# Seven weight slots laid out with high and low part side by side, each starting 64 bytes further modulo 512

## The chip, the cores and the metric

The kernel runs on one core of a Trainium2 chip. The metric is the device time of one execution in microseconds (us). Three runs of the kernel before gave 1726.82, 1725.1 and 1726.75 us, median 1726.75 us.

## The reference, cut to what matters

Two model blocks of two layers each work on one sequence of 256 tokens with 1024 channels in float32. Almost all the work is the product of activations with weight matrices that are used once each:

```python
for l in range(DEPTH):                       # first block
    proj = x @ w_in[l]
    ...                                      # recurrent mixer and sparse attention
    mix = jnp.concatenate([o_a, o_b], axis=-1) @ w_out[l]
    x = layer_norm(ALPHA * x + mix, ln1_g[l], ln1_b[l])
    ffn = (jax.nn.silu(x @ w_ffn_gate[l]) * (x @ w_ffn_up[l])) @ w_ffn_down[l]
    x = layer_norm(ALPHA * x + ffn, ln2_g[l], ln2_b[l])
```

The second block has the same outline, with three kinds of attention, gated branches (`gates[:, :, 0] * (o_mla @ w_branch[0]) + ...`), a feed-forward part with a short convolution, and a last gate.

## The kernel before, in words

**Weights as a stream.** All weights are cut into units of 128 partitions x 1024 float32 values, in the order in which they are used. A ring of seven slots (`RING`, L37) holds them. SyncE loads unit u into slot u mod 7 of `raw` (L625). ScalarE writes its high part, rounded to fp32r, to `w_hi` (L682). VectorE, for five slots of seven, and GpSimd, for two, write the low part `raw - w_hi` to `w_lo` (L686). A slot is 4096 bytes of a partition in each of the three tensors.

**Each product three times.** Activations are kept in a high and a low part too (`x_t_hi` and `x_t_lo`, and likewise `o_t`, `hs`, `n_t`, `c_t`, `pe`). TensorE adds high x high, high x low and low x high in PSUM. Every matmul of this kernel is a weight load (LDWEIGHTS, the stationary operand, 128 columns) and a matmul that streams the moving operand past it. There are two forms:

- `feature_major` (matmul on L720): the weights are stationary, 128 columns of a slot; the moving operand is a 256-column slice of `x_t` or `o_t`. 24 matmuls for a unit.
- `token_major` (matmul on L737): the activations are stationary; the moving operand is the weight slot, mostly 512 columns at a time. 12 matmuls for a unit.

```python
for k, (a, b) in enumerate(((w_hi, hi), (w_lo, hi), (w_hi, lo))):
    ...
    for kt in range(n, n + 4):
        mm = pe.matmul(target, a[:, i, w0 + kt * P:w0 + (kt + 1) * P], b[:, k0 + kt, :],
```

A feed-forward part runs gate and up units feature-major with `x_t` and down units token-major with `hs` as the stationary operand. The first matmul of a unit releases an older slot to ScalarE (`unit_begun`), and a finished low part releases the slot of `raw` to the next load. This order of work is written out by hand, and the change leaves it alone.

**Where things lie.** `sb` (L312) gives each tensor the next address of the partition, rounded up to 64 bytes. `raw`, `w_hi`, `w_lo`, `x`, 32 bytes of padding (L331), `x_t_hi`, `x_t_lo`, 32 bytes of padding (L334), then the constants and all others follow each other. A slot is 4096 bytes, so all seven slots, high and low, begin at one and the same address modulo 512. Every slice that the two forms of matmul read inside a slot (but for those of the 416- and 280-column units) and inside an activation tensor also begins a whole multiple of 512 bytes further. Counted from the weight slots and modulo 512, `x_t` lies at 32, `o_t` at 128, and `hs`, `n_t`, `c_t` and `pe` at 256.

In each form the address of the moving operand less that of the stationary one, modulo 512, is called the distance here. Before the change it is one number for a pair of tensors:

| matmul | moving less stationary |
|---|---|
| L720, `x_t` over weights | 32 |
| L720, `o_t` over weights | 128 |
| L737, weights over `x_t` | 480 |
| L737, weights over `o_t` | 384 |
| L737, weights over `hs`, `n_t`, `c_t`, `pe` | 256 |

Of the kernel before, what the change touches and what calls it, by code (L numbers as in the profile page):

```python
# [19 lines left out]
F32R = mybir.dt.float32r  # L20
# [4 lines left out]
P = 128  # L25
# [11 lines left out]
RING = 7  # L37
UNIT = 1024
# [264 lines left out]
def program(nc, stream, x_in, consts_in, onehot_in, rb_in, flip_in, param1_in, rows1_in,  # L303
# [5 lines left out]
    with ctx:  # L309
        top = [nc.sbuf_base + (-nc.sbuf_base) % 64]  # L310

        def sb(name, shape, dtype=F32, at=None):  # L312

            size = 4 * int(np.prod(shape[1:]))
            if at is None:
                at = top[0]
                top[0] += size + (-size) % 64
            assert at + size <= nc.sbuf_usable_end, (name, at + size)
            return nc.alloc_sbuf_tensor_at(name, shape, dtype, offset=at)
# [5 lines left out]


        raw = sb("raw", [P, RING, UNIT])
        w_hi = sb("w_hi", [P, RING, UNIT], F32R)
        w_lo = sb("w_lo", [P, RING, UNIT], F32R)
        x = sb("x", [P, T, D])  # L330
        top[0] += 32  # L331
        x_t_hi = sb("x_t_hi", [P, KT, S], F32R)
        x_t_lo = sb("x_t_lo", [P, KT, S], F32R)
        top[0] += 32  # L334
        consts = sb("consts", [P, N_CONST])
        ones = sb("ones", [P, P])
        mean_ones = sb("mean_ones", [P, P])
# [2630 lines left out]
```

## Time and profile before

| | us |
|---|---|
| median of 3 runs | 1726.75 |
| the profiled execution, its own time | 1727.11 |
| span of that execution | 1725.3 |
| TensorE matmul busy | 1653.6 (96%) |
| TensorE weight load busy | 1504.2 (87%) |
| VectorE busy | 1170.4 (68%) |
| ScalarE busy | 921.4 (53%) |
| GpSimd busy | 441.4 (26%) |

The profile's page gives busy time, shares of the chain that ended last, and groups of equal instructions. TensorE's matmuls overlap in the records: a matmul's own duration includes the time that its results take to drain, so durations add up to more than the span. The pace of a stream of matmuls is read from the timeline, as the difference of two start times divided by the number of matmuls that start in between.

### The profile page before, as it was taken

What the parts mean: (1) busy time and instruction counts of PE and PEld (TensorE: products, weight loads), DVE (VectorE), ACT (ScalarE), POOL (GpSimd) and SP (SyncE); (2) the same over time, 40 slices, a digit from 0 to 9 for tenths busy, and PEclk for the clock granted to TensorE, in tenths of its full rate; (3) what the DMA queues carried; (4) which work ended last, traced back from release to release, by engine and by line L of the source; (5) the groups of instructions that cost most, each with busy time, mean ns of one, the idle gap of its engine ahead of it and who ended that gap; (6) DMA issues with size and microseconds to landing.
All of it is one profiled execution on the core that took longest, in us unless ns stands there. A gap on an engine that the chain in (4) does not pass through costs nothing.

```text
span 1725.3 us, 30143 instructions
## 1 busy us (share of the span) xinstructions
PE 1653.6 (96%) x11354; PEld 1504.2 (87%) x11354; DVE 1170.4 (68%) x1601; ACT 921.4 (53%) x1576; POOL 441.4 (26%) x184
## 2 busy tenths in 40 slices
PE   8989999999988999999999999999999999999997
PEld 6878799989887899978899989999788999899996
DVE  5687754467786545476884877666767856777677
ACT  5664554446645544465655564545755555554445
POOL 2212122212121322224511132222235211222222
PEclk9999999999999999999999999999999999999999
DMA  9432455646523665546333455655554333466653
GB/s 332 157 119 96 161 199 185 201 147 210 162 78 122 220 193 188 191 153 213 113 110 100 140 199 184 215 185 182 180 194 146 110 100 116 161 218 199 207 183 127
DMA packets 82563, 288.74 MB, mean 167 GB/s; under 512 B 9051, under 2 KB 11908, under 8 KB 81924
## 3 DMA queue, kind: packets, MB, share of 16 engines
q1 hardware_dynamic: 77352, 272.58, 48.1%
q10 hardware_dynamic: 5084, 14.37, 2.5%
q8 instruction: 91, 1.49, 0.4%
q14 instruction: 36, 0.29, 0.1%
HBM read 284.81 MB, written 2.11 MB: 166 GB/s over the span
## 4 chain that ended last, share of the span: by engine, by line
PE 62%; DVE 7%; ACT 3%; issue 2%; DVEq 0%; ACTq 0%
PE bank L720 30%; PE bank L737 25%; PE bank L1294 2%; DVE w_lo L686 2%; PE bank L1275 1%; PE bank L1266 1%; ACT w_hi L682 1%; PE bank L765 1%; PE bank L1254 1%; PE bank L1307 0%; DVE qk L2528 0%; PE bank L1186 0%; PE bank L774 0%; PE bank L910 0%; DVE z L2502 0%
## 5 line engine op out<-in xcount | busy, mean ns | idle before, releaser
L686 POOL TENSOR_TENSOR w_lo<-raw,w_hi 128x1024 fp32r<-128x1024 f32 x146 | 375.3, 2570 | 1175.7 <-ACT w_hi L682 1175.7
L686 DVE TENSOR_TENSOR w_lo<-raw,w_hi 128x1024 fp32r<-128x1024 f32 x364 | 558.2, 1558 | 153.9 <-ACT w_hi L682 151.5
L682 ACT ACTIVATE w_hi<-raw 128x1024 fp32r<-128x1024 f32 x510 | 520.0, 1052 | 101.6 <-PE bank L737 46.3
L720 PE MATMUL bank<-x_t_hi,w_hi 128*128 128x256 f32 x1984 | 321.4, 284 | 5.3 <-ACT gl L1430 2.9
L720 PE MATMUL bank<-x_t_hi,w_lo 128*128 128x256 f32 x1984 | 313.9, 280 | 0.0
L720 PE MATMUL bank<-x_t_lo,w_hi 128*128 128x256 f32 x1984 | 313.5, 280 | 0.0
L720 PEld LDWEIGHTS bank<-x_t_hi,w_hi 128*128 128x128 f32 x1984 | 273.9, 190 | 16.8 <-issue 5.1
L720 PEld LDWEIGHTS bank<-x_t_hi,w_lo 128*128 128x128 f32 x1984 | 268.7, 189 | 0.0
L720 PEld LDWEIGHTS bank<-x_t_lo,w_hi 128*128 128x128 f32 x1984 | 268.2, 189 | 0.0
L737 PE MATMUL bank<-w_hi,x_t_hi 128*128 128x512 f32 (+3 forms) x448 | 136.1, 387 | 9.4 <-issue 5.8
L737 PE MATMUL bank<-w_hi,x_t_lo 128*128 128x512 f32 (+3 forms) x448 | 133.5, 381 | 1.5 <-DVE x_t_lo L1962 1.5
L737 PE MATMUL bank<-w_lo,x_t_hi 128*128 128x512 f32 (+3 forms) x448 | 133.2, 380 | 0.0
L737 PE MATMUL bank<-w_hi,hs_hi 128*128 128x512 f32 x352 | 109.4, 392 | 4.0 <-ACT hs_hi L1875 4.0
L737 PE MATMUL bank<-w_lo,hs_hi 128*128 128x512 f32 x352 | 108.9, 390 | 0.0
L737 PE MATMUL bank<-w_hi,hs_lo 128*128 128x512 f32 x352 | 108.7, 390 | 0.0
L737 PEld LDWEIGHTS bank<-w_hi,x_t_hi 128*128 128x128 f32 x448 | 81.2, 191 | 31.0 <-issue 14.0
L737 PEld LDWEIGHTS bank<-w_hi,x_t_lo 128*128 128x128 f32 x448 | 82.4, 190 | 19.3 <-DVE x_t_lo L1962 3.4
L737 PEld LDWEIGHTS bank<-w_lo,x_t_hi 128*128 128x128 f32 x448 | 83.1, 191 | 16.3
L1871 ACT ACTIVATE gs<-cv 128x256 f32<-128x256 f32 x44 | 18.4, 419 | 145.9 <-DVE cv L2676 145.9
L737 PEld LDWEIGHTS bank<-w_lo,hs_hi 128*128 128x128 f32 x352 | 66.1, 188 | 14.6
L737 PEld LDWEIGHTS bank<-w_hi,hs_lo 128*128 128x128 f32 x352 | 66.1, 188 | 14.3
L2363 DVE TENSOR_TENSOR hs_lo<-hs,hs_hi 128x256 fp32r<-128x256 f32 x36 | 15.3, 425 | 86.6 <-ACT hs_hi L1654 86.6
(390 smaller groups left out, 2128.0 us busy)
## 6 DMA issues: line engine op xcount, KB each, us to landing
raw<-stream SPq DMA_DIRECT2D x511, 512.0 KB, 4.3
rows<-rows ACTq DMA_DIRECT2D x4, 1024.0 KB, 4.6
gain<-rows ACTq DMA_DIRECT2D x8, 512.0 KB, 4.6
hv_p<-hv_dram ACTq DMA_DIRECT2D x14, 256.0 KB
x<-x_in SPq DMA_DIRECT2D x2, 512.0 KB, 5.0
bias_r<-rev_dram SPq DMA_DIRECT2D x1, 1024.0 KB, 7.3
hv_dram<-hv ACTq DMA_DIRECT2D x2, 512.0 KB, 7.4
y_out<-x SPq DMA_DIRECT2D x2, 512.0 KB, 2.7
```

Of the source, the lines that this page charges most:

```text
L682: self.eng.activation(w_hi[:, i, :], raw[:, i, :], ACT.Copy).then_inc(hi_done.sem, 1)
L686: self.eng.tensor_tensor(w_lo[:, i, :], raw[:, i, :], w_hi[:, i, :].bitcast(F32), ALU.subtract).then_inc((lo_pool if self.part == "pool" e ...
L720: mm = pe.matmul(target, a[:, i, w0 + kt * P:w0 + (kt + 1) * P], b[:, k0 + kt, :], start=kt + k == 0, stop=k == 2 and kt == kts - 1)
L737: mm = pe.matmul(target, a[:, kt0 + j, t * P:(t + 1) * P], b[:, i, j * width + c0:j * width + c0 + cn], start=first and j + k == 0, stop=l ...
L765: mm = pe.transpose(b[:, k * P:(k + 1) * P], source[:, t, (4 * h + k) * P:(4 * h + k + 1) * P], ident)
L1254: mm = pe.matmul(bank[banks.bank(at, f"s{i + half}")][:, t * S:(t + 1) * S], q[:, t * P:(t + 1) * P], k, start=True, stop=True)
L1266: mm = pe.matmul(b[:, t * S:(t + 1) * S], mq_t[:, h, t * P:(t + 1) * P], mk_t[:, h, :], start=True, stop=True)
L1275: mm = pe.transpose(b[:, m * P:(m + 1) * P], z2[:, i % 4, m * P:(m + 1) * P], ident)
L1294: mm = pe.matmul(bank[b0 + t][:, o], p_t2[:, i % 2, m * P:(m + 1) * P], v, start=kk == 0, stop=kk == 1)
L1871: act.activation(gs2[:, i % 2, :], cv[:, i % 2, :], ACT.Gelu_apprx_tanh).then_inc(c["gate_silu"].sem, 1)
L2363: dve.tensor_tensor(hs_lo[:, i % TAIL, :], hs[:, i % 2, :], hs_hi[:, i % TAIL, :].bitcast(F32), ALU.subtract).then_inc(c["h_lo"].sem, 1)
```

## The change

```diff
         raw = sb("raw", [P, RING, UNIT])
-        w_hi = sb("w_hi", [P, RING, UNIT], F32R)
-        w_lo = sb("w_lo", [P, RING, UNIT], F32R)
+        w = sb("w", [P, RING, 2 * UNIT + 16], F32R)
+        w_hi, w_lo = w[:, :, 0:UNIT], w[:, :, UNIT:2 * UNIT]
         x = sb("x", [P, T, D])
-        top[0] += 32
         x_t_hi = sb("x_t_hi", [P, KT, S], F32R)
         x_t_lo = sb("x_t_lo", [P, KT, S], F32R)
-        top[0] += 32
         consts = sb("consts", [P, N_CONST])
```

A slot now holds 4096 bytes of high part, 4096 bytes of low part and 64 bytes of nothing, so that slot i begins 64 x i bytes further modulo 512. `x` moves up by 448 bytes, `x_t` by 416, all that follows by 384. `raw` stays. No instruction is added, removed or moved; only addresses differ. The distances become:

| matmul | moving less stationary, slots 0 to 6 |
|---|---|
| L720, `x_t` over weights | 448, 384, 320, 256, 192, 128, 64 |
| L720, `o_t` over weights | 0, 448, 384, 320, 256, 192, 128 |
| L737, weights over `x_t` | 64, 128, 192, 256, 320, 384, 448 |
| L737, weights over `o_t` | 0, 64, 128, 192, 256, 320, 384 |
| L737, weights over `hs`, `n_t`, `c_t`, `pe` | 384, 448, 0, 64, 128, 192, 256 |

## Rows read from the trace of the kernel before

**Rows 1.** The page: busy time, and the granted clock in 40 slices.
```profile
PE 1653.6 (96%) x11354; PEld 1504.2 (87%) x11354; DVE 1170.4 (68%) x1601; ACT 921.4 (53%) x1576; POOL 441.4 (26%) x184
...
PEclk9999999999999999999999999999999999999999
```

**Rows 2.** The page: shares of the chain that ended last, by engine.
```profile
PE 62%; DVE 7%; ACT 3%; issue 2%; DVEq 0%; ACTq 0%
```

**Rows 3.** Groups by line, TensorE: xcount | busy us, mean ns | idle before.
```profile
L720 PE MATMUL bank<-x_t_hi,w_hi 128*128 128x256 f32 x1984 | 321.4, 284 | 5.3 <-ACT gl L1430 2.9 <-ACT p_t L549 1.6 <-ACT x_t_hi L1419 0.7
L720 PE MATMUL bank<-x_t_hi,w_lo 128*128 128x256 f32 x1984 | 313.9, 280 | 0.0
L720 PE MATMUL bank<-x_t_lo,w_hi 128*128 128x256 f32 x1984 | 313.5, 280 | 0.0
L737 PE MATMUL bank<-w_hi,x_t_hi 128*128 128x512 f32 (+3 forms) x448 | 136.1, 387 | 9.4 <-issue 5.8 <-DVE w_lo L686 2.4 <-ACT x_t_hi L1419 0.8
...
L737 PE MATMUL bank<-w_hi,hs_hi 128*128 128x512 f32 x352 | 109.4, 392 | 4.0 <-ACT hs_hi L1875 4.0
...
L720 PE MATMUL bank<-o_t_hi,w_hi 128*128 128x256 f32 x192 | 30.9, 283 | 0.4 <-DVE o_t_lo L2394 0.3
```

**Rows 4.** Timeline at 600 us, TensorE: start us, us, what; L720 with x_t.
```profile
600.06 0.63 PE L720 MATMUL bank<-x_t_hi,w_lo 128*128 128x256 f32 x4
...
602.40 0.28 PE L720 MATMUL bank<-x_t_hi,w_hi 128*128 128x256 f32 x1
```

**Rows 5.** Timeline at 960 us, TensorE: L720 with o_t.
```profile
960.11 0.64 PE L720 MATMUL bank<-o_t_lo,w_hi 128*128 128x256 f32 x4
...
962.49 0.28 PE L720 MATMUL bank<-o_t_hi,w_lo 128*128 128x256 f32 x1
```

**Rows 6.** The chain that ended last in order of time: start us, us, what.
```profile
953.37 34.47 PE bank L720 x288
...
1176.09 16.80 PE bank L720 x144
```

**Rows 7.** Timeline at 1000 us, TensorE: L737 with x_t stationary.
```profile
999.80 0.63 PE L737 MATMUL bank<-w_hi,x_t_lo 128*128 128x512 f32 x2
...
1002.60 0.63 PE L737 MATMUL bank<-w_hi,x_t_lo 128*128 128x512 f32 x2
```

**Rows 8.** Timeline at 186 us, TensorE: L737 with o_t stationary.
```profile
186.16 0.62 PE L737 MATMUL bank<-w_hi,o_t_hi 128*128 128x512 f32 x2
...
188.96 0.39 PE L737 MATMUL bank<-w_hi,o_t_hi 128*128 128x512 f32 x1
```

**Rows 9.** Timelines at 1519 and 1012 us, TensorE: L737 with hs and pe stationary.
```profile
1519.55 0.62 PE L737 MATMUL bank<-w_lo,hs_hi 128*128 128x512 f32 x2
...
1521.83 0.63 PE L720 MATMUL bank<-x_t_hi,w_hi 128*128 128x256 f32 x4
...
1011.86 0.62 PE L737 MATMUL bank<-w_hi,pe_lo 128*128 128x512 f32 x2
...
1014.58 0.62 PE L737 MATMUL bank<-w_hi,pe_lo 128*128 128x512 f32 x2
```

**Rows 10.** Timeline at 836 us, TensorE: short matmuls, dv over p_t.
```profile
836.73 1.06 PE L1294 MATMUL bank<-dv,p_t 128*128 128x128 f32 x8
837.63 0.60 PE L1186 MATMUL bank<-consts,sqn 128*128 128x128 f32 x4
```

**Rows 11.** Instructions of tile w_hi: xcount: duration ns min/median/max, first and last start.
```profile
L682 ACT ACTIVATE w_hi<-raw x510: 1037/1047/1109, 6.6 to 1719.8; 128x1024 fp32r<-128x1024 f32 x170
...
L686 DVE TENSOR_TENSOR w_lo<-raw,w_hi x364: 1209/1225/3456, 7.7 to 1721.6; 128x1024 fp32r<-128x1024 f32 x182
...
L686 POOL TENSOR_TENSOR w_lo<-raw,w_hi x146: 2352/2454/3417, 11.8 to 1721.0; 128x1024 fp32r<-128x1024 f32 x146
```

## The prediction, written before the changed kernel had run

> **What bounds the kernel now.** The page first. TensorE's matmuls are busy for 1653.6 us of 1725.3 us, at a granted clock whose 40 slices all read 9, so nearly always the 2.4 GHz level [rows 1]. The chain that ended last is mostly TensorE, 62% of the span, with 12% on other engines and on issue [rows 2]. So what each of TensorE's streaming matmuls takes more or less reaches the end nearly whole, while time won on VectorE, ScalarE or GpSimd reaches it only through the few waits. Next the groups by line. L720 with `x_t` runs 3 x 1984 = 5952 matmuls of 256 columns; L737 runs 3 x 448 = 1344 with `x_t` stationary (1056 of them 512 columns wide, the rest narrower) and 3 x 352 = 1056 with `hs` stationary; L720 with `o_t` runs 3 x 192 = 576 [rows 3]. The reader should see how many there are: 1 ns on each of the 5952 is 6.0 us, 0.35% of the time.
>
> The change moves addresses and nothing else, so it can act only if the pace of an instruction depends on where its operands lie. The trace of before shows five distances between moving and stationary operand, and paces for them (start to start, over a run of matmuls that wait for nothing else):
>
> - L720, `x_t`, distance 32: 20 matmuls in 602.40 - 600.06 = 2.34 us, 117.0 ns [rows 4]; 144 in 16.80 us, 116.7 ns [rows 6].
> - L720, `o_t`, distance 128: 20 in 2.38 us, 119.0 ns [rows 5]; 288 in 34.47 us, 119.7 ns, which holds the changes of bank too [rows 6].
> - L737, distance 480: 12 in 2.80 us, 233.3 ns [rows 7].
> - L737, distance 384: 12 in 2.80 us, 233.3 ns [rows 8].
> - L737, distance 256: 10 in 2.28 us, 228.0 ns with `hs`, and 12 in 2.72 us, 226.7 ns with `pe` [rows 9].
>
> The same shape on the same engine takes 2 ns more or 6 ns more between these rows. Address is one thing in which they differ, the producer of the stationary tensor and the stage another. I take the address to be the likelier reason, since the shapes are equal and the streams wait for nothing.
>
> **The change part by part.**
>
> *L720 with `x_t`, 5952 matmuls.* The distance goes from 32 to 64, 128, 192, 256, 320, 384 and 448, a seventh of the units each. Only 128 has a row: 2.0 ns above distance 32 (119.0 less 117.0) [rows 4, 5]. The bounds are both ends of what rows show: all seven stay at 117.0, nothing; all seven come to 119.0, 5952 x 2.0 = +11.9 us. Below that, a distance could be better than 32: the floor is then the pace of a matmul that is short enough to leave only the weight load, 8 in 837.63 - 836.73 = 0.90 us, 112.5 ns [rows 10], and all seven there would be 5952 x 4.5 = -26.8 us. I take the middle between the two rows for this same form, +1.0 ns: 5952 x 1.0 = +6.0 us.
>
> *L737 with `x_t` stationary, 1056 wide matmuls.* From 480 to 64, 128, ... 448. Of the seven, 256 has 227 ns and 384 has 233 ns; 448 lies between two distances that both have 233 ns (384 and 480), so 233; the four others have no row and get the middle, 230. Mean (227 + 2 x 233 + 4 x 230) / 7 = 230.4 ns, 2.9 ns below now: 1056 x 2.9 = -3.1 us. Bounds: nothing, and -6.6 x 1056 = -7.0 us if all reach 226.7.
>
> *L737 with `hs` stationary, 1056 matmuls.* These lie at 256 now, the best distance that a row shows, and go to 384, 448, 0, 64, 128, 192 and 256. By the same figures (0 counted as unknown) the mean is (2 x 233 + 227 + 4 x 230) / 7 = 230.4 ns, against 228.0: 1056 x 2.4 = +2.5 us. Bounds: nothing, and +5.3 x 1056 = +5.6 us.
>
> *Distance 0.* Slot 2 over `hs`, and slot 0 with `o_t`, now begin together modulo 512. The short matmuls of `dv` over `p_t` have both operands at 384 modulo 512, distance 0, and run at 112.5 ns [rows 10]. So I price no special penalty for it.
>
> *The remaining matmuls on weights* (`o_t`, `n_t`, `c_t`, `pe` and the narrow ones, some 1300) start from 128, 256, 384 and 480 and land on the same mixture: zero, with 2 ns x 1300 = 2.6 us to either side.
>
> *ScalarE, VectorE and GpSimd on the slots.* They read `raw`, which stays, and write `w_hi` and `w_lo` at new addresses. ScalarE's 510 take 1037 to 1109 ns, VectorE's have minimum 1209 and median 1225 ns for the same 1024 elements [rows 11]; the long ones are GpSimd and VectorE in each other's way, which does not hang on addresses. Cost zero. TensorE is the cover: GpSimd and VectorE are idle for 74% and 32% of the span [rows 1]. If VectorE's 364 each took 50 ns more, 18 us of its time, nearly all would lie under TensorE.
>
> *Loads.* `raw` and the source stay where they are, so the 511 stream loads are unchanged. The transposes of `x` over the identity matrix come to distance 0; there are 64 and the row above speaks for no change.
>
> **Sum.** +6.0 - 3.1 + 2.5 = +5.4 us, of which some 90% lie on the path (where TensorE waits for another engine anyway, its pace is free): +4.9 us. The profiled execution took 1727.11 us, 0.36 us above the median of the three runs, so I forecast 1726.75 + 4.9, about 1731.5 us, 0.3% slower. The measurement can tell about 0.2%, 3.5 us, from no change, so this is a small effect close to that border.
>
> **The rivals.**
>
> *Rival A, faster: spreading gets most slots out of each other's way.* Weight load and moving stream of TensorE disturb each other only near certain distances, and 32 is one of them; 117.0 against the 112.5 ns of the short ones would be the price paid now. With the slots spread over seven distances, five in seven run at 112.5 ns: 5952 x 4.5 x 5/7 = -19.1 us, and the wide matmuls over `x_t` gain 3 us, `hs` loses 2.5: about 1707 us. For it: 112.5 ns is what the weight load alone needs, so 4.5 ns are there to be explained. Against it: distance 128 is a row of before and is slower, not faster, than 32 [rows 4, 5], and 226.7 against 233.3 ns shows that wide streams differ by distances which are all multiples of 64 or near one. Milder forms (two slots in seven gain) give 1718 us. Chance 0.3.
>
> *Rival B, no change: pace does not depend on the distance.* Then the differences between rows come from stage and form. For it: ScalarE and VectorE show flat durations whatever TensorE reads [rows 11], and distance 0 costs nothing at 112.5 ns [rows 10]. The time stays within 3 us of 1726.75. Chance 0.32. The Trainium skill speaks for this rival and so against any effect of the change: in "TensorE: Matmul & The Clock Gate", section "What happens when you issue a matmul", the weight load and the moving operand have SBUF read ports of their own, and loading the next weights takes nothing from the running matmul; "SBUF — State Buffer", section "Who interferes with whom", adds that TensorE waits on nobody. By that rule the sum would be 0. The rows do not settle it: equal shapes at 226.7 and 233.3 ns ask for some cause that the rule leaves no room for.
>
> *Rival C, clearly slower: what matters is the remainder modulo 64.* `x_t` lies 32 bytes off a multiple of 64 now and would come to rest on one, like `o_t`. All 5952 would take 119.0 ns: +11.9 us, and the wide ones over `x_t` would stay at 233, with `hs` unchanged at 228: 1739 us. It decides as soon as the offset of 32 is what makes `x_t` quicker than `o_t`. For it: `x_t` is the only moving operand off a multiple of 64, and it has the quickest 256-column row. Chance 0.15, part of the slower cases.
>
> **How the numbers follow.** Forecast with its neighbourhood (slower by over 3.5 us, up to 8 us) 0.23, Rival A 0.3, Rival B 0.32, Rival C 0.15. The forecast is the sum's own value; since cases of both signs hold most of the chance and the effect is small, the likeliest one's own range is 1729 to 1736 us. The range reaches from Rival A in its strong form, a little below 1707, to the bounds of the slower terms added, 11.9 + 5.6 = 17.5 us above now: 1704 to 1744 us. Outside stays a gain on all slots (1700 or less) or a penalty at a distance that no row shows. Faster by over 0.2%: 0.30. Within 0.2%: 0.32. Slower by over 0.2%: 0.38.
>
> **What the profile of the changed kernel would show.** The timeline of L720 with `x_t` should run at different paces in units of different slots, 117 to 119 ns, mean 118; equal paces of 117 in all units mean Rival B, 112 to 114 in most mean Rival A, 119 in all mean Rival C. L737 over `x_t` should come from 233 to about 230 ns, L737 over `hs` go from 228 to about 230 ns. Durations of L682 and L686, counts of instructions and the granted clock should not move. The prediction is wrong if the time moves without the pace of L720, for instance through waits of TensorE on L686, or if one slot alone (slot 2 over `hs`) carries the loss.

## The result, and the profile after

| | before | after |
|---|---|---|
| median of 10 runs, us | 1726.78 | 1733.25 |
| span of the profiled execution, us | 1725.3 | 1731.2 |
| TensorE matmul busy, us | 1653.6 | 1659.2 |

The ratio is 1.0038, with a 95% interval of 1.0028 to 1.0047: the changed kernel is 6.5 us slower by the medians. The forecast was 1731.5 us.

The page of the changed kernel, busy time, granted clock and the chain, against [rows 1, 2]:

```profile
PE 1659.2 (96%) x11354; PEld 1507.2 (87%) x11354; DVE 1168.7 (68%) x1601; ACT 921.0 (53%) x1576; POOL 440.9 (25%) x184
...
PEclk9999999999999999999999999999999999999999
...
PE 63%; DVE 7%; ACT 2%; issue 2%; DVEq 0%; ACTq 0%
```

Counts of instructions and the clock's digits are as they were; the mean granted clock was 0.986 before and 0.988 after. VectorE, ScalarE and GpSimd are busy for 0.4 to 1.7 us less; TensorE alone is busy for longer, by 5.6 us, and the span is longer by 5.9 us. Names are shorter now (`w` for both parts) and lines two lower: L718 is the old L720, L735 the old L737.

Six feed-forward units in a row, L718 with `x_t`, in the changed kernel's timeline of TensorE (start us, us, what). The units begin at 1181.36, 1184.22, 1187.05, 1189.90, 1192.72 and 1195.45 us and use slots 3, 4, 5, 6, 0 and 1:

```profile
1181.36 1.11 PE L718 MATMUL bank<-x_t_hi,w 128*128 128x256 f32 x8
...
1184.22 1.11 PE L718 MATMUL bank<-x_t_hi,w 128*128 128x256 f32 x8
...
1187.05 1.11 PE L718 MATMUL bank<-x_t_hi,w 128*128 128x256 f32 x8
...
1189.90 1.10 PE L718 MATMUL bank<-x_t_hi,w 128*128 128x256 f32 x8
...
1192.72 1.07 PE L718 MATMUL bank<-x_t_hi,w 128*128 128x256 f32 x8
...
1195.45 1.10 PE L718 MATMUL bank<-x_t_hi,w 128*128 128x256 f32 x8
...
1198.29 0.63 PE L735 MATMUL bank<-w,hs_hi 128*128 128x512 f32 x2
```

A unit is 24 matmuls, so each difference divided by 24 is a pace: 119.2 ns at distance 256, 117.9 at 192, 118.8 at 128, 117.5 at 64, 113.8 at 448, 118.3 at 384. Same instructions, same engine, no wait between them, and paces from 113.8 to 119.2 ns in units of different slots. In [rows 4] 20 matmuls ran at 117.0. The down units follow suit. One over `hs` at distance 384 and one at 64:

```profile
591.07 1.09 PE L735 MATMUL bank<-w,hs_hi 128*128 128x512 f32 x4
...
593.86 1.11 PE L718 MATMUL bank<-x_t_hi,w 128*128 128x256 f32 x8
...
599.54 1.09 PE L735 MATMUL bank<-w,hs_hi 128*128 128x512 f32 x4
...
602.30 1.07 PE L718 MATMUL bank<-x_t_hi,w 128*128 128x256 f32 x8
```

2.79 us and 2.76 us for 12 matmuls, 232.5 and 230.0 ns, against 228.0 in [rows 9].

Below, "mean pace" is the mean difference between the starts of two successive matmuls of a form on the same pair of tensors in the whole trace, where gaps more than 60 ns above the streaming time (over 167 ns for 256 columns, over 273 ns for 512) are left out: waits, and the stretches at the 1.2 GHz level, where a matmul of 256 columns starts every 213 to 214 ns. By it, the change did this:

| form | matmuls | before, ns | after, ns | us |
|---|---|---|---|---|
| L720, `x_t` | 5952 | 116.8 | 117.7 | +5.4 |
| L737, `x_t`, 512 wide | 1056 | 233.3 | 231.6 | -1.9 |
| L737, `hs` | 1056 | 228.5 | 231.7 | +3.4 |
| sum | | | | +6.9 |

The last column is matmuls times difference, from paces before rounding. The changes of all other matmuls on weights cancel to less than 0.1 us. The pace of TensorE's matmuls accounts for the whole 6.5 us.

Runs of one kernel scatter by several us, and the granted clock goes with it: of the ten runs of the changed kernel the two with a mean clock of 0.990 took 1731.3 and 1731.4 us, and the one with 0.983 took 1736.7 us. Over 93 runs that list a clock (the changed kernel, the experiments with several runs, and the kernel before beside them), a clock lower by 0.001 goes with 0.6 us more inside one kernel (an estimate, by a straight line through them).

### The profile page after: what moved, and what is told of

It is laid out like the page before. It is cut to its first block, busy times and chain, and to the rows that moved or that the text cites. A ratio compares the mean times of both kernels' runs of the same rounds, so it can differ in the third digit from the quotient of the medians.

```text
span 1731.2 us, 30143 instructions
## 1 busy us (share of the span) xinstructions
PE 1659.2 (96%) x11354; PEld 1507.2 (87%) x11354; DVE 1168.7 (68%) x1601; ACT 921.0 (53%) x1576; POOL 440.9 (25%) x184
## 4 chain that ended last, share of the span: by engine, by line
PE 63%; DVE 7%; ACT 2%; issue 2%; DVEq 0%; ACTq 0%
PE bank L718 30%; PE bank L735 25%; DVE w L684 2%; PE bank L1292 2%; PE bank L1273 1%; PE bank L1264 1%; ACT w L680 1%; PE bank L763 1%; PE bank L1252 1%; PE bank L1305 0%; DVE qk L2526 0%; PE bank L908 0%; PE bank L916 0%; PE bank L1184 0%; PE bank L772 0%
## 5 line engine op out<-in xcount | busy, mean ns | idle before, releaser
L684 POOL TENSOR_TENSOR w<-raw,w 128x1024 fp32r<-128x1024 f32 x146 | 374.9, 2568 | 1184.6 <-ACT w L680 1184.6
L684 DVE TENSOR_TENSOR w<-raw,w 128x1024 fp32r<-128x1024 f32 x364 | 556.9, 1554 | 154.7 <-ACT w L680 152.8
L680 ACT ACTIVATE w<-raw 128x1024 fp32r<-128x1024 f32 x510 | 520.1, 1052 | 105.7 <-PE bank L735 45.3
L718 PE MATMUL bank<-x_t_hi,w 128*128 128x256 f32 x3968 | 556.7, 283 | 5.3 <-ACT gl L1428 3.0
L718 PEld LDWEIGHTS bank<-x_t_hi,w 128*128 128x128 f32 x3968 | 509.1, 189 | 17.7 <-issue 5.4
L718 PE MATMUL bank<-x_t_lo,w 128*128 128x256 f32 x1984 | 314.7, 281 | 0.0
L718 PEld LDWEIGHTS bank<-x_t_lo,w 128*128 128x128 f32 x1984 | 269.0, 189 | 0.0
L735 PE MATMUL bank<-w,x_t_hi 128*128 128x512 f32 (+3 forms) x896 | 232.6, 382 | 9.6 <-issue 5.8
L735 PEld LDWEIGHTS bank<-w,x_t_hi 128*128 128x128 f32 x896 | 162.7, 191 | 46.2 <-issue 14.2
L735 PE MATMUL bank<-w,hs_hi 128*128 128x512 f32 x704 | 192.1, 394 | 3.7 <-ACT hs_hi L1873 3.7
L735 PEld LDWEIGHTS bank<-w,hs_hi 128*128 128x128 f32 x704 | 127.2, 188 | 28.2 <-issue 4.0
L735 PE MATMUL bank<-w,x_t_lo 128*128 128x512 f32 (+3 forms) x448 | 132.7, 379 | 1.7 <-DVE x_t_lo L1960 1.7
L735 PE MATMUL bank<-w,hs_lo 128*128 128x512 f32 x352 | 109.7, 393 | 0.0
L735 PEld LDWEIGHTS bank<-w,x_t_lo 128*128 128x128 f32 x448 | 82.3, 190 | 19.5 <-DVE x_t_lo L1960 4.0
L735 PEld LDWEIGHTS bank<-w,hs_lo 128*128 128x128 f32 x352 | 66.1, 188 | 15.5
L718 PE MATMUL bank<-o_t_hi,w 128*128 128x256 f32 x384 | 53.6, 282 | 0.7 <-DVE o_t_lo L2392 0.7
L718 PEld LDWEIGHTS bank<-o_t_hi,w 128*128 128x128 f32 x384 | 48.8, 189 | 1.1 <-DVE o_t_lo L2392 1.1
```

Of the source, the lines that this page charges most:

```text
L680: self.eng.activation(w_hi[:, i, :], raw[:, i, :], ACT.Copy).then_inc(hi_done.sem, 1)
L684: self.eng.tensor_tensor(w_lo[:, i, :], raw[:, i, :], w_hi[:, i, :].bitcast(F32), ALU.subtract).then_inc((lo_pool if self.part == "pool" e ...
L735: mm = pe.matmul(target, a[:, kt0 + j, t * P:(t + 1) * P], b[:, i, j * width + c0:j * width + c0 + cn], start=first and j + k == 0, stop=l ...
```

## The experiments

The theory: the pace depends on the distance between the operands' addresses, and on little else that the change touches. Every run changes addresses alone, by padding. `rest` stands for all tensors behind `x_t`.

**High and low part side by side, without the stagger.**

```diff
-        w_hi = sb("w_hi", [P, RING, UNIT], F32R)
-        w_lo = sb("w_lo", [P, RING, UNIT], F32R)
+        w = sb("w", [P, RING, 2 * UNIT], F32R)
+        w_hi, w_lo = w[:, :, 0:UNIT], w[:, :, UNIT:2 * UNIT]
```

> High and low part side by side, but without the 64 bytes of stagger and with both paddings of 32 bytes kept, so that every distance (moving less stationary operand, modulo 512) is that of the kernel before. Theory of distances: the pace of L720 with x_t stays at 116.8 ns and the time at 1726.8 us, within 2 us. Rival (the slot's layout itself costs the time, by the 28672 bytes from high to low part that become 4096, or by what ScalarE and VectorE write): the whole loss of the change, 1733 us, shows here.

Measured: 1727.6 us against 1727.35 us for the kernel before on the same chip, ratio 1.0001 (0.9992 to 1.0010). Mean paces 116.8, 233.4 and 228.5 ns, those of before. The new layout of a slot costs nothing that these runs can tell (the interval stays within 1.7 us); the stagger and the paddings taken out, that is the distances, carry the loss.

**One other distance for all slots.** In the next three runs only the two paddings around `x_t` change, so that `x_t` moves and the rest stays at its place modulo 512.

```diff
         x = sb("x", [P, T, D])
-        top[0] += 32
+        top[0] += 192
         x_t_hi = sb("x_t_hi", [P, KT, S], F32R)
         x_t_lo = sb("x_t_lo", [P, KT, S], F32R)
-        top[0] += 32
+        top[0] += 384
```

> The kernel before with x_t put 192 bytes behind the weight slots modulo 512 instead of 32, all else at its old place modulo 512. In the changed kernel the units at distance 192 had the quickest pace of L720 with x_t, 115.4 ns, and those of L737 over x_t at 320 had 230.5 ns. Theory of distances: 5952 x (115.4 - 116.8) = -8.3 us and 1056 x (230.5 - 233.3) = -3.0 us, so 1715.5 us, faster than both kernels. Rival (unequal slots disturb each other through their sequence, not through the distance of each): the pace does not follow, and the time stays within 3 us of 1726.8.

Measured: 1723.84 us against 1727.35, ratio 0.9984 (0.9974 to 0.9993). It is faster than both kernels, but by a third of what was expected. L737 over `x_t` came to 229.2 ns, better than expected; over `hs`, whose distance had not changed, to 226.8 from 228.5; L720 over `x_t` stayed at 116.8 ns, where 115.4 had been expected. The unit means show why: of the 248 units with this distance some run at 114 ns a matmul and more at 118, and few between (single matmuls: 23% at 113 or 114 ns, 67% at 117 or 118). The changed kernel's 115.4 ns had been such a mixture too, with more of the quick ones.

> The same with x_t 256 bytes behind the slots. In the changed kernel the units at distance 256 had the slowest pace of L720 with x_t, 119.7 ns, and 229.8 ns in L737 over x_t. Theory of distances: 5952 x (119.7 - 116.8) = +17.3 us, 1056 x (229.8 - 233.3) = -3.7 us, so 1740.4 us. Rival as for the run before: 1726.8 us, within 3.

(paddings 256 and 320.) Measured: 1736.93 us, ratio 1.0056 (1.0042 to 1.0070), slower by 9.6 us. L720 over `x_t` 119.8 ns as expected, in 9 of 10 matmuls exactly 120; L737 over `x_t` 227.5 ns, better than the 229.8 expected.

> The same with x_t 160 bytes behind the slots, like the 32 of the kernel before no multiple of 64. Theory that the pace is a smooth function of the distance modulo 512: L720 with x_t lies between the 118.5 ns of distance 128 and the 115.4 ns of 192, at about 117 ns, and the time at 1726 us, within 4. Rival C of the prediction (what matters is being 32 bytes off a multiple of 64): 116.8 ns exactly as at distance 32, and all multiples of 64 alike, which the changed kernel's paces from 115.4 to 119.7 ns already speak against.

(paddings 160 and 416.) Measured: 1736.12 us, ratio 1.0050 (1.0036 to 1.0064). L720 over `x_t` 118.6 ns, L737 233.5 ns. Both readings fail. 160 is 32 off a multiple of 64 and yet slow, which rules Rival C out. And the pace is not about 117 ns, between its neighbours 128 (118.5 ns) and 192 (115.4 ns) in the changed kernel, but as slow as the slower of them.

The chain in order of time shows these paces in one row each, because it holds the same stretch in every kernel: 144 matmuls of L720 with `x_t`, and 96 of L737 over `x_t`. The kernel at distance 192, then the one at 256 and the one at 160 (start us, us, what):

```profile
986.49 21.99 PE bank L737 x96
...
1176.23 16.96 PE bank L720 x144
```

```profile
996.62 21.80 PE bank L737 x96
...
1186.92 17.27 PE bank L720 x144
```

```profile
995.70 22.41 PE bank L737 x96
...
1185.58 17.09 PE bank L720 x144
```

144 matmuls take 16.96 us (117.8 ns; this stretch ran at the slower of the two paces of distance 192), 17.27 us (119.9) and 17.09 us (118.7), against 16.80 us in [rows 6].

**Does the place itself count, or other engines' addresses?**

```diff
         raw = sb("raw", [P, RING, UNIT])
+        top[0] += 192
         w_hi = sb("w_hi", [P, RING, UNIT], F32R)
```

> 192 bytes of padding ahead of w_hi in the kernel before, so that every tensor but raw lies 192 bytes further and no distance on TensorE changes. Theory of distances: pace of L720 with x_t 116.8 ns, of L737 over x_t 233.3 ns, time 1727 us. Rival (what counts is where an operand itself begins modulo 512, or where ScalarE and VectorE write against what they read from raw): other paces, at the least 1 ns off on L720, and L682 or L686 of other durations.

One run took 1729.68 us, where the kernel before took 1730.38 us beside it. Mean paces 116.9, 233.3 and 228.5 ns. ScalarE's and VectorE's durations on the slots, in the view of tile `w_hi`, are those of [rows 11] within 2 ns but for VectorE's longest; GpSimd's median is 27 ns longer:

```profile
L683 ACT ACTIVATE w_hi<-raw x510: 1037/1047/1111, 6.5 to 1722.5; 128x1024 fp32r<-128x1024 f32 x170
...
L687 DVE TENSOR_TENSOR w_lo<-raw,w_hi x364: 1207/1225/3467, 7.6 to 1724.3; 128x1024 fp32r<-128x1024 f32 x182
L687 POOL TENSOR_TENSOR w_lo<-raw,w_hi x146: 2378/2481/5143, 12.4 to 1723.6; 128x1024 fp32r<-128x1024 f32 x146
```

A common shift of both operands by 192 bytes changes no pace, while 64 bytes between them do: of the two, it is the difference between TensorE's operands that counts. Other common shifts were not tried by themselves.

**The period.**

> x_t 288 bytes behind the slots, 256 more than before. If the pattern repeats every 512 bytes (what the stagger supposes), the pace of L720 with x_t is free to be any; if it repeats every 256 bytes, as the changed kernel's paces at 64 and 320 (117.5 and 117.7 ns) and at 128 and 384 (118.5 and 118.7 ns) suggest, it is 116.8 ns as at 32, L737 over x_t 233.3 ns, and the time 1727 us.

(paddings 288 and 288.) 1727.83 us in one run, against 1730.38 us beside it. Mean paces 116.8, 233.3 and 228.5 ns: those of distance 32 to the last digit. For this distance 256 bytes more change nothing, so the pattern seems to repeat every 256 bytes, not only every 512. The slots of the changed kernel mostly agree: over `x_t` 117.5 and 117.7 ns at 64 and 320, 118.5 and 118.6 ns at 128 and 384. At 192 and 448 they had 115.4 and 117.2 ns, mixtures of two paces in which 192 had more quick units (23 of 38 against 6 of 36). The chain's rows of this kernel are those of before, 16.80 and 22.39 us:

```profile
988.62 22.39 PE bank L737 x96
...
1176.90 16.80 PE bank L720 x144
```

Seven slots staggered by 64 bytes thus use only four distances: in L720 over `x_t`, two slots each at 64, 128 and 192, and one at 0.

> x_t 96 bytes behind the slots. Smooth theory: between 117.5 ns (64) and 118.5 ns (128) on L720, 118 ns, about 1732 us. Rival C (32 bytes off a multiple of 64 is what helps): 116.8 ns. Distance 160 had 118.6 ns, so Rival C is expected to fail here too.

(paddings 96 and 480.) 1746.63 us in one run, against 1730.38 us for the kernel before beside it; span 1744.8 us, 19.5 us longer than that of the profile before. It is the slowest distance found. L720 120.1 ns, in single matmuls anything from 116 to 125; L737 over `x_t` 234.3 ns, over `hs` 229.9 ns. Both expectations miss: it is worse than either neighbour.

```profile
1190.50 17.28 PE bank L720 x144
```

> x_t 224 bytes behind the slots, between the 116.8 ns that distance 192 had in a kernel with one distance for all and the 119.8 ns of 256. Smooth theory: 118.3 ns on L720 and 228 to 229 ns on L737 over x_t, about 1731 us. If distances of the form 32 below a multiple of 256 behave as 32 above one does (two streams that pass each other at the same lag), 116.8 ns and about 1722 us.

(paddings 224 and 352.) 1736.84 us in one run, against 1730.38 us beside it. L720 118.3 ns as the smooth theory had it; L737 over `x_t` 233.3 ns instead of 228 to 229.

**Half steps.** All paddings so far are multiples of 32 bytes. For steps of 16 the slots themselves were put 16 bytes into a larger tensor, with paddings 128 and 384 for the first of the two runs and 160 and 352 for the second.

```diff
-        w_hi = sb("w_hi", [P, RING, UNIT], F32R)
-        w_lo = sb("w_lo", [P, RING, UNIT], F32R)
+        w = sb("w", [P, 2 * RING * UNIT + 16], F32R)
+        w_hi, w_lo = (w[:, a:a + RING * UNIT].rearrange("p (i n) -> p i n", i=RING) for a in (4, 4 + RING * UNIT))
```

> Weight slots begin 16 bytes later, x_t 176 bytes behind them, 16 below the 192 at which the units of L720 turned out to run in one of two states, 113 to 114 or 118 ns a matmul, apparently set when a unit begins. hs comes to distance 272, o_t to 112. If the lag between weight load and stream decides which state holds, a distance beside 192 may hold the quick one: 114 ns, 5952 x (114 - 116.8) = -16.7 us on L720, about 1708 us. Smooth theory: between 118.6 ns (160) and 116.8 ns (192), 117.7 ns, and about 1730 us.

1739.3 us in one run, against 1730.45 us for the kernel before beside it; L720 over `x_t` 118.7 ns, over `hs` (distance 272) 231.7 ns.

> The same with x_t 208 bytes behind the slots, 16 above 192. Quick state held: 114 ns on L720, about 1708 us. Smooth theory: between 116.8 ns (192) and 118.3 ns (224), 117.5 ns, and about 1729 us.

1742.76 us in one run, against the same 1730.45 us; L720 over `x_t` 119.0 ns, L737 over `x_t` 233.3 ns, over `hs` 231.8 ns. Neither holds the quick state, and both are slower than the smooth theory said. The idea that a distance beside 192 fixes the quick state is wrong for these two. (Both move the slots by 16 bytes and `hs` to distance 272 as well, so their times are not those of `x_t` alone.)

**Only `hs` and `o_t` moved.**

```diff
         x_t_lo = sb("x_t_lo", [P, KT, S], F32R)
-        top[0] += 32
+        top[0] += 96
```

> The kernel before with the second padding 96 instead of 32 bytes, so that everything behind x_t moves by 64 and x_t stays: L737 over hs comes from distance 256 to 192, L720 with o_t from 128 to 192. The changed kernel's units over hs at 192 had 233.5 ns, those of o_t at 192 had 116.8 ns. Theory of distances, with additive terms: 1056 x (233.5 - 228.5) = +5.3 us and 576 x (116.8 - 118.8) = -1.2 us, L720 with x_t at 116.8 ns as before, time 1731 us, slower by 0.24%. Rival (the loss of the changed kernel came from x_t alone, the paces over hs were an echo of it): 1727 us, over hs 228.5 ns.

Measured: 1734.14 us against 1726.16 us, ratio 1.0038 (1.0025 to 1.0052). Over `hs` 232.7 ns (+4.3 ns, +4.5 us), L720 with `o_t` 115.5 ns from 118.8 (-1.9 us), L720 over `x_t` 116.8 as before. A down unit of this kernel:

```profile
1104.86 0.62 PE L737 MATMUL bank<-w_hi,hs_hi 128*128 128x512 f32 x2
...
1107.64 0.63 PE L720 MATMUL bank<-x_t_hi,w_hi 128*128 128x256 f32 x4
```

12 in 2.78 us, 231.7 ns, against 228.0 in [rows 9]. So the term over `hs` is real without any move of `x_t`. The time lost, 6.6 us by the ratio, is more than the 2.3 us of these paces (4.5 less 1.9, less 0.3 for L737 over `o_t`); `n_t`, `c_t` and `pe`, which moved too, add 0.9 us. Part of the rest goes with the clock: the five runs had a mean granted clock of 0.9854, the 14 of before that count 0.9881, worth 1.6 us by the estimate above. In the profiled execution some single waits of TensorE differ by about 1 us from those of before, both ways: longer at 103 (`hid`), 174 (`am`), 490 (`q_e`) and 1474 us (`o_t`), shorter at 753 (`x_t`) and 951 us (transposes of `o`). What decides these isn't settled; several of them appear in the kernel below too, which is faster. In sum TensorE was not busy for 75.5 us of the span here, and for 71.7 us before.

**The version that the paces point to.** `x_t` at 192, `o_t` at 192 (448), `hs` at 256.

```diff
         x = sb("x", [P, T, D])
-        top[0] += 32
+        top[0] += 192
...
-        top[0] += 32
+        top[0] += 128
         consts = sb("consts", [P, N_CONST])
...
+        top[0] += 64
         o_base = top[0]
         o_t_hi = sb("o_t_hi", [P, 12, S], F32R)
         o_t_lo = sb("o_t_lo", [P, 12, S], F32R)
+        top[0] += 192
         dist = sb("dist", [P, T, S])
```

> The best version that the paces point to: x_t 192 bytes behind the slots as in the run of 1723.8 us, o_t at 448, which by the period of 256 is 192 again, hs at 256. Theory of distances: L720 with x_t 116.8 ns, L737 over x_t 229.2 ns, over hs 226.8 ns, L720 with o_t from 118.8 to 116.8 ns (-1.2 us), so 1722.7 us, 0.2% below the kernel before. If o_t adds nothing: 1723.8 us. If units with x_t stay in their quick state of 113 to 114 ns, more, down to 1705 us, but nothing here is made to hold it.

Measured: 1724.96 us against 1726.16, ratio 0.9984 (0.9973 to 0.9995), the same as with `x_t` alone. L720 over `o_t` ran at 113.4 ns, the quick state in nearly all units, 5.4 ns below before where 2 were expected; its timeline:

```profile
955.15 0.62 PE L722 MATMUL bank<-o_t_hi,w_lo 128*128 128x256 f32 x4
...
957.42 0.62 PE L722 MATMUL bank<-o_t_hi,w_hi 128*128 128x256 f32 x4
```

20 matmuls in 2.27 us, 113.5 ns. Over 576 matmuls that is 3.1 us, and little of it arrives. The chain in order of time says where it goes. Before, this stretch was one piece, 288 matmuls in 34.47 us from 953.37 to 987.84 us [rows 6]. Now:

```profile
954.57 16.62 PE bank L722 x144
971.20 0.02 issue
971.22 0.43 DVE merged_b L2627
971.64 1.69 DVE merged L2632
...
981.51 2.35 DVE w_lo L688 x2
983.86 0.33 DVE merged L2627
984.20 2.30 DVE x_t_lo L2614
...
986.89 1.65 PE bank L722 x12
988.54 11.67 PE bank L739 x51
```

In the middle of the stretch the chain leaves TensorE for VectorE, which merges the branches and splits weights and is now the later of the two. The stretch takes 988.54 - 954.57 = 33.97 us, 0.50 us less than before, for 288 x 5.4 ns = 1.56 us of quicker matmuls.

Over the whole kernel two more things eat into the gain. In this profiled execution TensorE was not busy for 77.1 us of the span (76.1 us in that with `x_t` alone at 192), against 71.7 us before. And the granted clock was lower: 0.9847 on the average of the 11 runs against 0.9881 for the kernel before, worth 2.0 us by the estimate above. One of its drops in the timeline:

```profile
1031.50 0.79 PE L739 MATMUL bank<-w_hi,hs_hi 128*128 128x512 f32 x2 [2.29 <-ACT hs_hi L1877]
1032.09 1.05 PE L739 MATMUL bank<-w_lo,hs_hi 128*128 128x512 f32 x2
1032.95 1.05 PE L739 MATMUL bank<-w_hi,hs_lo 128*128 128x512 f32 x2
1033.80 1.05 PE L739 MATMUL bank<-w_hi,hs_hi 128*128 128x512 f32 x2
```

TensorE has waited 2.29 us, the granted clock from 1032.0 to 1035.4 us is 0.50, the level of 1.2 GHz, and a matmul starts every 425 ns. In the kernel before the same unit follows a wait of 2.00 us, the clock stays at 1.00, and the pace is 225 ns. In all, the matmuls on weights in such stretches took 12.8 us more here than they would have at the upper level, against 10.3 us before (an estimate, with 117, 173, 190 and 230 ns for the widths 256, 384, 416 and 512). Whether the change of addresses brings these drops about, by moving the waits, was not tested.

**All distances, in one table** (modulo 256, mean pace in kernels with one distance for all slots; `x_t` is the activation unless another is named):

| distance | L720, 256 columns, ns | L737, 512 columns, ns |
|---|---|---|
| 0 | 119.8 | 226.8 to 230.1 (`hs`), 227.5 (`x_t`) |
| 16 | | 231.7 and 231.8 (`hs`) |
| 32 | 116.8 | 233.3 |
| 48 | | 233.3 |
| 64 | | 229.2 |
| 80 | | 231.1 |
| 96 | 120.1 | 233.5 |
| 112 | 120.0 and 118.4 (`o_t`) | |
| 128 | 118.8 (`o_t`) | 232.4 (`o_t`) |
| 160 | 118.6 | 234.3 |
| 176 | 118.7 | |
| 192 | 116.8 (`x_t`), 115.5 and 113.4 (`o_t`) | 232.7 (`hs`) |
| 208 | 119.0 | |
| 224 | 118.3 | 233.3 |

## Why the prediction was right

**The bound and the kind of effect: right.** The prediction said that only TensorE's pace could carry the change and that L720 over `x_t`, 5952 times, would decide the sign. TensorE's busy time rose by 5.6 us, and the terms of pace add to 6.9 us against 6.5 us measured. The prediction held this with little confidence: its own neighbourhood had a chance of 0.23, less than Rival A or Rival B.

**L720 over `x_t`, +6.0 us: right in size, by +5.4 us, though not by its reasoning.** It took the middle between 117 and 119 ns. The slots spread wider than these bounds, mean paces 115.4 ns (192) to 119.7 ns (256) in the changed kernel, and the mean over seven happened to be near the middle. That was luck.

**L737 over `x_t`, -3.1 us: right in sign, too large.** It came to 231.6 ns instead of 230.4, -1.9 us. The guess of 230 for four distances without a row was 1.3 ns low on the average: they had 230.1 (64), 232.0 (128), 232.6 (192) and 230.5 (320). At 256 the units had 229.8, not 227. The three errors in size partly cancel: the sum was 5.4 us and the paces give 6.9 us.

**L737 over `hs`, +2.5 us: right in sign, too small,** +3.4 us. The run that moves `hs` alone confirms that it is a loss of its own.

**Distance 0 without a penalty: half right.** From a short matmul no price could be read. Over `hs` slot 2, at 0, had 229.6 ns, the quickest of the seven; with `x_t` moving, the slowest pace of the seven, 119.7 ns, was slot 3's, whose 256 is 0 again by the period found.

**Other engines, loads, transposes at nothing: right.** L680 has a mean of 1052 ns as L682 had, L684 on VectorE 1554 after 1558, and the stream's loads a median of 4.3 us as before.

**90% on the path.** For losses it is about right: the pace terms of the run at distance 256 add to 17.7 - 6.2 + 0.3 = 11.8 us, and 9.6 us arrived; at 96 it was 21.7 us and 19.5 us of span. For gains it is not: with `x_t` at 192 the terms add to -6.5 us and 3.5 us arrived, with `o_t` too to -10.3 us and about 2.8 us arrived by the ratio. The prediction used one share for both signs. Part of the difference is the granted clock, lower in both: 0.9856 against 0.9872 with `x_t` at 192 (about 1 us), 0.9847 against 0.9881 with `o_t` too (about 2 us). Another part is TensorE's idle time, 4.4 and 5.4 us longer in their profiles, where it waits for other engines.

**The rivals.** Rival A (most slots reach the floor) failed: only part of the units of two distances reached 113 to 114 ns. Rival B (pace does not depend on distance) failed by the paces in one timeline, and by the runs at 256, 160 and 96: moving `x_t` by 64 bytes, from distance 32 to 96, changes the pace by 3 ns in 117. The Trainium skill says in "TensorE: Matmul & The Clock Gate", section "What happens when you issue a matmul", that loading the next weights takes no read bandwidth from the running matmul. Taken as a rule on time, as the prediction did for this rival, it does not hold in this stream of fp32r matmuls; whether it is the reading of the two operands that collides, no run here shows. Rival C (multiples of 64 are slow, 32 off them is quick) failed by 96, 160 and 224, which are 32 off and slow.

## What to carry to other kernels

In a kernel that streams weight loads and matmuls back to back, the address of the moving operand less that of the stationary one, modulo 256 bytes, is a knob worth some tenths of a per cent here: the worst distance for `x_t` took 16 us more than the kernel before beside it (0.9%, one run each), the best 3.5 us less (0.2%). Try it with one padding and read the pace of a known stretch from the chain or the timeline of a single profile, which shows 0.1 ns where run times scatter by several us; at a distance with two paces, take the mean over many units. Don't spread slots over many distances unasked: that bought the average of all here, and this kernel, whose one distance was among the good ones, lost by it. Compare the granted clocks of two sets of runs before putting a difference of 2 us down to the change.

## What had not been expected of the hardware

- The pattern repeats after 256 bytes where that was tried alone: distances 32 and 288 give 116.8 ns both, with 233.3 ns for both in L737.
- At the 1.2 GHz level the distance makes no difference. The matmuls of 256 columns with `x_t` that fell into such stretches (17 to 74 of them in each of the 14 profiles) have a mean pace of 213.1 to 213.7 ns in every kernel, at whatever distance.
- There are two states for one and the same distance. At 192 most units of 24 matmuls run either at 114 or at 118 ns a matmul, as the changed kernel's units at 448 (113.8 ns) and at 192 (117.9 ns) do above; with `o_t` nearly all units were quick (113.4 ns) in one kernel and fewer (115.5 ns) in another with the same distance modulo 256. What sets the state was not found.
- The pace over `hs` depends on where `x_t` lies. `hs` at distance 256 had 228.5 ns behind units of `x_t` at 32 and 226.8 ns behind units at 192, though nothing of its own had changed. With `x_t` at 96 and 224 it had 229.9 and 230.1 ns, and in the changed kernel the same distance had 231.2 ns, 1.6 ns more than slot 2 at 0. How one stream hands its pace to the next was not tried.
- That the weight load and the moving operand meet is inferred from the difference of their addresses; which part of the chip makes them meet was not tried and is left open. ScalarE, VectorE and GpSimd show no part in it: 192 bytes between `raw` and everything behind it changed no pace.
